# Attention groups on one Trainium2 core: the products with v of a pair of heads move behind the scores of the next pair

## The reference

```python
NSA_HEADS, NSA_GROUPS, NSA_HPG, NSA_DH = 16, 4, 4, 64

q = q_nsa.reshape(B, S, NSA_GROUPS, NSA_HPG, NSA_DH)
kv = kv_nsa.reshape(B, S, 6, NSA_GROUPS, NSA_DH)
o_cmp, p_cmp = nsa_compressed(q, kv[:, :, 0], kv[:, :, 1], ...)
top_i, top_ok = nsa_select(p_cmp, S)
o_slc = nsa_selected(q, kv[:, :, 2], kv[:, :, 3], top_i, top_ok)
o_win = nsa_window(q, kv[:, :, 4], kv[:, :, 5])
gb = jax.nn.sigmoid(g_nsa.reshape(B, S, NSA_GROUPS, NSA_HPG, 3))
y_nsa = gb[..., 0:1] * o_cmp + gb[..., 1:2] * o_slc + gb[..., 2:3] * o_win
...
# each branch, per head: p = masked_softmax(q @ k.T * scale), o = p @ v
...
gm = jax.nn.sigmoid(g_merge.reshape(B, S, N_BRANCH, D_MODEL))   # g_merge = h @ part of w_in
```

## Time and profile before

| what | value |
|---|---|
| median of 3 runs | 2795.47 us (2791.68 to 2801.25) |
| the profiled execution | 2792.84 us, of which the span is 2791.0 us |
| TensorE busy in the span | 2734.3 us (98%) |
| VectorE, ScalarE busy | 2057.8 us (74%), 1223.6 us (44%) |
| granted TensorE clock, mean | 0.993 of full speed |
| the attention loop | 342 to 667 us of the span, four groups of about 80 us |
| TensorE, VectorE, ScalarE busy in the loop | 297.4, 231.2, 222.1 of 325 us |

### The profile page before, as it was taken

How to read it: one execution, slowest core, us unless ns; L and a number is a source line. 1 busy time by engine, 2 the same in 40 slices (tenths; PEclk the granted TensorE clock), 3 DMA queues, 4 the chain that set the end, 5 groups by cost and what they waited for, 6 DMA issues and landing times.

```text
span 2791.0 us, 41188 instructions
## 1 busy us (share of the span) xinstructions
PE 2734.3 (98%) x16368; PEld 2406.4 (86%) x16368; DVE 2057.8 (74%) x2974; ACT 1223.6 (44%) x1787; POOL 7.1 (0%) x6
## 2 busy tenths in 40 slices
PE   8999999999999999999999999999999999999998
PEld 7878877777888989889898899988999888889897
DVE  5456576666668969689695797876979588669795
ACT  4343476665343434434244343432434356434342
POOL 0000000000000000000000000000000000000000
PEclk9999999999999999999999999999999999899999
DMA  7223222223532333333332233232333343123332
GB/s 225 92 79 106 99 81 78 86 86 127 197 115 82 106 106 106 112 100 106 106 101 98 79 106 118 91 119 68 116 106 102 120 170 112 61 76 106 107 106 76
DMA packets 270515, 295.41 MB, mean 106 GB/s; under 512 B 6339, under 2 KB 256339, under 8 KB 267663
## 3 DMA queue, kind: packets, MB, share of 16 engines
q1 hardware_dynamic: 268784, 287.82, 31.7%
q10 hardware_dynamic: 1566, 5.27, 0.5%
HBM read 276.30 MB, written 16.78 MB: 105 GB/s over the span
## 4 chain that ended last, share of the span: by engine, by line
PE 71%; DVE 21%; issue 4%; ACT 2%; DVEq 0%; DMA 0%; ACTq 0%; SPq 0%
PE bank L1519 12%; PE bank L1521 12%; PE bank L1520 12%; PE bank L1992 5%; PE bank L1994 5%; PE bank L1993 5%; DVE gate_quarters_lo L2844 2%; DVE up_quarters_lo L2844 2%; PE bank L1815 1%; PE bank L2167 1%; DVE w_lo L2287 1%; PE bank L1534 1%; PE bank L1536 1%; PE bank L1535 1%; PE bank L1897 1%
## 5 line engine op out<-in xcount | busy, mean ns | idle before, releaser
L2287 DVE TENSOR_TENSOR w_lo<-w_raw,w_hi 128x2048 fp32r<-128x2048 f32 (+2 forms) x164 | 338.9, 2068 | 133.9 <-ACT w_hi L891 129.7
L891 ACT ACTIVATE w_hi<-w_raw 128x2048 fp32r<-128x2048 f32 (+2 forms) x134 | 242.2, 1814 | 237.7 <-PE bank L1521 158.3
L1519 PE MATMUL bank<-hid_hi,w_hi 128*128 128x512 f32 x816 | 317.9, 390 | 0.0
L1520 PE MATMUL bank<-hid_lo,w_hi 128*128 128x512 f32 x816 | 317.5, 389 | 0.0
L1521 PE MATMUL bank<-hid_hi,w_lo 128*128 128x512 f32 x816 | 317.5, 389 | 0.0
L1519 PE MATMUL bank<-h_hi,w_hi 128*128 128x512 f32 x736 | 292.2, 397 | 2.5 <-DVE w_lo L2287 1.7
L1521 PE MATMUL bank<-h_hi,w_lo 128*128 128x512 f32 x736 | 286.6, 389 | 0.0
L1520 PE MATMUL bank<-h_lo,w_hi 128*128 128x512 f32 x736 | 286.6, 389 | 0.0
L1521 PEld LDWEIGHTS bank<-hid_hi,w_lo 128*128 128x128 f32 x816 | 153.2, 188 | 31.9
L1520 PEld LDWEIGHTS bank<-hid_lo,w_hi 128*128 128x128 f32 x816 | 153.2, 188 | 31.4
L1519 PEld LDWEIGHTS bank<-hid_hi,w_hi 128*128 128x128 f32 x816 | 153.2, 188 | 31.3
(11 more groups left out here) (502 smaller groups left out, 6994.1 us busy)
## 6 DMA issues: line engine op xcount, KB each, us to landing
w_raw<-in_ffn_w_in_dram SPq DMA_DIRECT2D x88, 1024.0 KB, 5.0
w_raw<-in_ffn_w_out_dram SPq DMA_DIRECT2D x32, 1024.0 KB, 5.2
w_raw<-in_w_ffn_in_dram SPq DMA_DIRECT2D x22, 1024.0 KB, 5.0
w_raw<-in_w_in_dram SPq DMA_DIRECT2D x20, 1024.0 KB, 5.4
w_raw<-in_w_in_dram SPq DMA_DIRECT2D x24, 512.0 KB, 4.0
w_raw<-in_ffn_w_out_dram SPq DMA_DIRECT2D x16, 768.0 KB, 4.5
w_raw<-in_conv_w_pw_dram SPq DMA_DIRECT2D x12, 1024.0 KB, 6.5
phase_taps<-in_conv_dw_phases_dram SPq DMA_DIRECT2D x10, 1152.0 KB, 7.8
```

Of the source, the lines that this page charges most:

```text
L891: nc.scalar.activation(w_hi[SLOT[u]][:, 0:n], raw[s][:, 0:n], ACT.Copy).then_inc(w_hi_ready, 1)
L1519: nc.tensor.matmul(bank[b][:, 0:n], wh, xh, start=first, stop=False)
L1520: nc.tensor.matmul(bank[b][:, 0:n], wh, xl, start=False, stop=False)
L2287: v.tensor_tensor(w_lo[slot][:, 0:n], raw[s][:, 0:n], w_hi[slot][:, 0:n].bitcast(F32), ALU.subtract).then_inc(w_lo_ready, 1)
```

## The change

In iteration `m`, TensorE weighed pair `k = m - 3` at the end, after that pair's own `turn` and six gate products. Now iteration `m` weighs pair `k - 1`, after the scores of pair `m` and ahead of the `turn` of pair `k`; the last pair is weighed after the loop. The instructions are the same ones, with the same semaphores; only their order on TensorE differs. VectorE's, ScalarE's and SyncE's code is as it was.

```diff
@@ -1907,15 +1907,16 @@
                         scores(2 * m + 1)
                     if m == 0:
                         pe.wait_ge(m_lo_s, 4)
+                    if k >= 1:
+                        weigh(k - 1)
                     if k >= 0:
                         turn(2 * k)
                         turn(2 * k + 1)
                     gates(GATE_PAIR[m])
-                    if k >= 0:
-                        weigh(k)
                     if m < PAIRS and k % PAIRS_PER_BLOCK == PAIRS_PER_BLOCK - 1:
                         cmp_turn((k + 1) // PAIRS_PER_BLOCK)
                 gates(GATE_TILES * 3 * KT)
+                weigh(PAIRS - 1)
```

## The result

| | median of its runs | lowest to highest | group of the loop | ratio to before, 95% interval |
|---|---|---|---|---|
| before (five runs) | 2795.47 us | 2791.68 to 2804.55 | 80.0 us | |
| changed (five runs) | 2772.10 us | 2769.75 to 2778.95 | 74.5 us | 0.9917 [0.9893, 0.9941] |

The changed kernel is 23.4 us faster, 0.83%. A group is counted from its first scores to those of the next; the loop's first group takes 1.1 to 1.5 us more than the others in every kernel and is left out of this column. The profiled execution of the changed kernel took 2769.75 us, of which the span is 2767.9 us, 23.1 less than before. A second set of six runs of the same kernel gave 2771.35 us, ratio 0.9906 [0.9885, 0.9928].

The account below looks back on a forecast made before the run. The prediction took TensorE's waits in the attention loop, before the products with v, as the bound. Scores 19.2 plus compressed transposes 2.2 less new waits 1.4 made 20.0 us, from 2795.5 to 2775.5 us; range 2767 to 2787.

Parts of the forecast that it names:

- The bound: In the attention loop TensorE loses time to waits, not throughput; 33.7 us is lost before the products with v.
- Reading from start to start: Waits before products with v, taken between starts: 22.4 us in pairs 0 to 11, against some 15 by rows' ends.
- The scores as cover: Scores of 0.71 or 0.48 us before products with v leave 0.80 of 5.61 us a group; 19.2 us gained.
- The compressed transposes: Earlier transposes shorten the wait at pair 4's second head by 0.55 us a group, 2.2 us in all.
- New waits: VectorE and ScalarE, with queues in strict order, cost 0.35 us a group, 1.4 us; bounds 0 and 5 us.
- Pairs 12 to 15: Their products with v come in iterations without scores, so their 2.54 us a group stay.
- The wait for masks and q's load: Scores waiting for masks cost 0; the next group's q load keeps its slack of 3.6 us.
- The loads' 50.3 us: In the loop's waits view, the loads' 50.3 us at L1897 and L1891 fall to about 29.
- A: VectorE or ScalarE sets the loop's pace and half is given back: 9.6 us gained, 2785.9 us; chance 0.12.
- B: Scores wait for late masks ahead of ready products with v: 12 us slower, 2808 us; chance 0.04.
- C: q's load or the loop's DMAs hold the group at 80 us: no gain, 2795.5 us; chance 0.03.
- D: Fewer waits spare the lower clock at 586 to 594 us, 3.1 us: 23.1 us gained, 2772.4 us; chance 0.12.

Follow-up runs that it names:

- low_earlier: From the changed kernel, VectorE makes the low part of the third gate weight in iteration 6 instead of 7: 2778.88 us in one execution, group 73.9 us.
- cmp_late3: From the changed kernel, the compressed transposes of iterations 6, 10 and 14 go back behind the products with v; scores stay ahead: 2784.71 us.
- cmp_only: From the kernel before, only the compressed transposes of iterations 6, 10 and 14 move ahead of the products with v: 2787.36 us.
- scores_half: From the changed kernel, the scores of a pair's second head go back behind the products with v; the first head's stay ahead: 2774.63 us.
- cmp_late: From the changed kernel, all four compressed transposes, the group's first included, go back behind the scores and products with v: 2786.48 us.
- low_last: From the changed kernel, VectorE makes the low part of the next group's first weight after pair 15's low part: 2763.99 us in one execution.
- best17: From the changed kernel, VectorE's weight low parts move from iterations 7 to 6 and 17 to 18, ScalarE's high part from 16 to 17: 2760.84 us.
- best18: As best17, but ScalarE's high part of the next group's first weight comes in iteration 18, behind pair 15's high part: 2764.03 us.
- best17_gates: From best17, one gate product less in iterations 4 and 5 and two more in iteration 18: 2759.51 us.

## Why the prediction was right, and where it was not

**The bound: right.** TensorE's waits were what could be won; VectorE's and ScalarE's busy times changed by 1 and 3 us and the time went down by the waits.

**Reading from start to start: right.** By the rows' ends 15 us were to be won and by starts 22.4 in pairs 0 to 11; the group's account closes with the starts (4.55 + 0.56 + 0.4 = 5.51 against 5.5) and not with the ends. The Trainium skill (Perfetto Trace Analysis, section "Summary: the profiler window per engine type") states that TensorE's recorded end is an estimate; the trace agrees, the ends lie 0.17 us past the next start in both kernels.

**The scores as cover: right in kind, the sum a little high.** Predicted 0.80 us left in pairs 0 to 11, measured 1.06 in the changed kernel. Pair 0 has 0.14 as forecast; pair 1 has 0 and not 0.09; pair 5 has 0.58 and not 0.39, pair 8 0.08 and not 0.18, and pairs 4 and 10 have 0.09 and 0.17 where none was forecast. 4.55 us a group against 4.81. That pair 5 would be the hard case was read from the right row; that it was VectorE's order, and not its load, came out with `low_earlier`.

**The compressed transposes: the mis-sized term.** The prediction gave them 0.55 us a group. They are worth 1.85 beside the scores (`cmp_late3`) and 2.1 alone (`cmp_only`), over three times as much. I counted the wait that I saw in the trace of before, 0.61 us at pair 4's second head. I didn't count that alone the transposes are cover for pairs 3, 7 and 11. Nor did I count that without their move the scores' own gain is 3.65 us and not 4.81, because the wait at pair 4's head would have grown to 1.32 and pair 12's from 0.39 to 0.83, and pair 12's scores would have come 0.4 late. That is the step of the prediction that failed. That the total came out near all the same (20.0 forecast, 22.2 by the groups) is in part luck: the scores' term was 1.2 to 1.4 us a group too high (3.65 us alone, 77.9 - 74.5 = 3.4 beside the transposes) and the other 1.3 to 1.55 too low.

**New waits: smaller than allowed for.** I took 0.35 us a group. Pairs 0 to 11 keep 0.26 us more than the count; against it stand the 0.4 us from the shorter blocks, which I had not seen. VectorE's idle time changed its place: 28.5 us for scores and 9.0 for ScalarE's high parts (its rows at L2596 and L2590 in the kernel before) became 22.7 for the high parts alone. Whether ScalarE would be the next to hold the loop back, no run shows.

**Pairs 12 to 15: right.** 2.54 became 2.55; within it pair 12 waits 0.22 less and pair 13 0.23 more. **The wait for masks and q's load: right,** no score product waits for a mask, VectorE's 28.5 us of waiting for scores shrank to nothing, and no wait for q has a row in the loop.

**The loads' 50.3 us: predicted about 29, measured 18.3.** The forecast's own terms add up to 30.0 (64 x 0.26 + 10.2 + 4 x 0.80) and not to 29. I kept 0.26 us for all 64 places, but a load that doesn't have to wait has no idle row at all. At the 40 places that vanished from the view that makes 10.4 us of the difference.

**The rivals.** A (half given back) is out: 1.06 us a group is left of 5.61. B is out at the lateness that this kernel has; with 0.68 us more of it its mechanism appears, 0.65 us a group, and is still far from making the kernel slower. C is out: nothing else held the group at 80 us. D gave 2772.4 us, which is closer to 2772.1 than my forecast, but not by its mechanism: it needed waits worth 20.0 us and 3.1 us of clock. The waits and blocks alone make 22.2 of the 23.4 us; for the other 1.2 the scatter of the runs leaves room enough. The profiled loop did gain 3.1 us of clock besides; but the changed kernel's next profile has such a stretch again, so it is no constant part of the difference.

## What to carry to other kernels

Where TensorE waits for a chain on other engines, write first whatever else is ready: the wait falls by about the duration of that cover, whether it is scores, gate products or transposes, until something else that the moved work was waiting for comes to light. Before sizing such a move, list everything that changes its place, and ask of each piece both whom it makes wait and whom it covers. Then read the rows just ahead of each wait that stays on the engine waited for: three pieces of weight preparation, not urgent where they stood, cost 2 us in each group. Moving them by one or two iterations brought 10.5 us by the medians of one set (2771.35 to 2760.84). Of these the loop and the wait at its end (1.9 us from start to start) explain 4 x 2.1 - 1.9 = 6.5; the rest is not shown to come from the move, since the clock behind the loop differed by as much (17.0 us lost in the one profile, 13.0 in the other).

## What the hardware showed beyond that

**The lower clock stays through a busy stretch.** By stretch (columns as above), the start of the second group in `low_earlier`, and of the third in `scores_half`:

```profile
424.00:440.00 16.00, 16.00 (x50) 13.48 (x49) 2.45 (x5) 0.00 (x0) 0.00 (x0) 0.50 0.12 33
```

```profile
500.00:516.00 16.00, 16.00 (x50) 13.44 (x49) 2.71 (x5) 0.00 (x0) 0.00 (x0) 0.50 0.13 33
```

The granted clock is 0.50, the level of 1.2 GHz, for all 16 us while TensorE is busy in every one of them. In `low_earlier` that group took 83.2 us and not 73.9. All such stretches inside the loop, in whichever profile, begin within a few microseconds of a group's start; in these kernels that is just behind the waits of pairs 14 and 15. Of the profiled executions of the ten kernels (or repeats) that have both waits at over 0.9 us, six show a stretch at a start of the second to fourth group (before, changed kernel again, `scores_half`, `cmp_late`, `cmp_late3`, `low_earlier`), four none. Of the four kernels in which one or both waits are gone (`low_last`, `best17`, `best18`, `best17_gates`) none does; two show one at 634 to 640 us, about where the loop ends and TensorE waits for the moved weight.

The Trainium skill (TensorE: Matmul & The Clock Gate, section "HAM oscillation — how this bites in real kernels") has the clock fall after idle gaps, in an example with longer gaps than these. The counts above go with that as to where it falls. That it stays down through 16 us in which TensorE never stands still, and that the same kernel has the stretch in one execution and not in the next, the rule doesn't explain, and four executions are too few to call the link shown. It is a practical matter all the same: the twelve runs of `cmp_late3`, with two of these stretches in its profile, go from 2772.9 us at a mean granted clock of 0.995 to 2796.8 at 0.985, and those of `best17` from 2759.7 at 0.995 to 2765.3 at 0.992. For most runs only this mean is known, so where in the program they lost it is not shown.

**A wait costs a little more than itself.** The first product behind a wait takes 0.17 us to the next start, where the same product without a wait takes 0.12; eight places in four groups make 1.6 us of this change's gain.
